# Two weight units' low halves computed on GpSimd instead of VectorE, in the first block's output projection

## What is computed

```python
def first_block(x, ...):
    h = x
    for layer in range(DEPTH):
        u = rms_norm(h, g_mix[layer])
        if layer % 2 == 0:      # 8 latent-attention heads and 8 stick-breaking heads
            h = h + mla_stick_breaking_mixer(u, ..., ev_w_out[i])
        else:
            h = h + chunk_band_mixer(u, od_w_qkv[i], od_rel_bias[i], od_w_out[i])
        u = rms_norm(h, g_ffn[layer])
        h = h + swiglu(u, w_gate[layer], w_up[layer], w_down[layer])
    return rms_norm(h, g_final)

# the end of mla_stick_breaking_mixer
    return jnp.concatenate([o_a, o_b], axis=-1) @ w_out
```

## Time and profile before

| what | value |
|---|---|
| median of 3 runs | 1110.11 us (1110.09 to 1110.68) |
| the profiled execution | 1109.47 us, its span 1107.7 us |
| mean granted TensorE clock | 0.991 |
| TensorE busy | 1078.0 us, 97% of the span |
| VectorE busy | 755.3 us, 68% |
| ScalarE busy | 578.0 us, 52% |
| GpSimd busy | 220.9 us, 20% |

### The profile page before, as it was taken

The page is one execution under the profiler, slowest core; times in us unless marked ns, Lnnn a source line. Parts: engine busy times, 40 slices in busy tenths (PEclk is TensorE's granted clock), DMA queues, the critical chain, the costliest instruction groups (busy, mean ns, idle before and its releaser), DMA issues.

```text
span 1107.7 us, 22257 instructions
## 1 busy us (share of the span) xinstructions
PE 1078.0 (97%) x8781; PEld 1053.5 (95%) x8781; DVE 755.3 (68%) x1233; ACT 578.0 (52%) x852; POOL 220.9 (20%) x202
## 2 busy tenths in 40 slices
PE   7998999999999999999999999999999989999997
PEld 7997999999999999999999899998899989999997
DVE  6677575555757766656555678987986657887652
ACT  5667554444545554644444544446666355555542
POOL 1431030000222110300000277785450000000000
PEclk9999999999999999999999999999999989999999
DMA  8734266657675343566555554453334534554451
GB/s 270 212 105 153 80 193 194 197 175 220 204 223 186 129 139 100 187 193 201 161 186 191 171 153 152 140 166 114 115 123 146 181 123 152 193 188 155 158 180 39
DMA packets 187941, 181.36 MB, mean 164 GB/s; under 512 B 17951, under 2 KB 186284, under 8 KB 187867
## 3 DMA queue, kind: packets, MB, share of 16 engines
q1 hardware_dynamic: 187323, 178.23, 50.9%
q0 software_dynamic: 544, 2.10, 0.7%
HBM read 179.27 MB, written 1.05 MB: 163 GB/s over the span
## 4 chain that ended last, share of the span: by engine, by line
PE 91%; DVE 4%; ACT 3%; issue 1%; DMA 0%; DVEq 0%; SPq 0%; ACTq 0%
PE ps L555 28%; PE ps L557 27%; PE ps L556 27%; DVE w_lo L394 1%; ACT w_hi L378 1%; PE ps L1981 1%; PE ps L2165 1%; PE ps L2103 1%; PE ps L1988 1%; PE ps L2172 1%; PE ps L2001 0%; PE ps L2000 0%; PE ps L1822 0%; PE ps L2127 0%; PE ps L1785 0%
## 5 line engine op out<-in xcount | busy, mean ns | idle before, releaser
L394 DVE TENSOR_TENSOR w_lo<-raw,w_hi 128x2048 fp32r<-128x2048 f32 (+3 forms) x157 | 333.4, 2137 | 137.6 <-ACT w_hi L378 137.4
L378 ACT ACTIVATE w_hi<-raw 128x2048 fp32r<-128x2048 f32 (+3 forms) x182 | 316.1, 1753 | 35.4 <-PE ps L557 25.3
L555 PE MATMUL ps<-u_hi,w_hi 128*128 128x256 f32 x944 | 265.1, 281 | 2.8 <-DVE w_lo L2343 2.3
L556 PE MATMUL ps<-u_lo,w_hi 128*128 128x256 f32 x944 | 262.4, 278 | 0.0
L557 PE MATMUL ps<-u_hi,w_lo 128*128 128x256 f32 x944 | 262.4, 278 | 0.0
L555 PE MATMUL ps<-m_hi,w_hi 128*128 128x258 f32 (+2 forms) x792 | 231.4, 292 | 6.6 <-DVE m_lo L524 4.2
L556 PE MATMUL ps<-m_lo,w_hi 128*128 128x258 f32 (+2 forms) x792 | 226.6, 286 | 0.0
L557 PE MATMUL ps<-m_hi,w_lo 128*128 128x258 f32 (+2 forms) x792 | 226.5, 286 | 0.0
L555 PEld LDWEIGHTS ps<-u_hi,w_hi 128*128 128x128 f32 x944 | 178.7, 189 | 4.0 <-DVE w_lo L2343 2.7
L556 PEld LDWEIGHTS ps<-u_lo,w_hi 128*128 128x128 f32 x944 | 178.6, 189 | 0.2
L557 PEld LDWEIGHTS ps<-u_hi,w_lo 128*128 128x128 f32 x944 | 178.6, 189 | 0.0
(11 more groups left out here) (364 smaller groups left out, 1681.0 us busy)
## 6 DMA issues: line engine op xcount, KB each, us to landing
raw<-in_w_in SPq DMA_DIRECT2D x24, 1024.0 KB, 5.3
raw<-in_w_gate SPq DMA_DIRECT2D x22, 1024.0 KB, 5.3
raw<-in_w_up SPq DMA_DIRECT2D x22, 1024.0 KB, 5.4
raw<-in_ffn_up SPq DMA_DIRECT2D x22, 1024.0 KB, 5.1
raw<-in_w_down SPq DMA_DIRECT2D x16, 768.0 KB, 4.6
raw<-in_od_w_qkv SPq DMA_DIRECT2D x12, 1024.0 KB, 5.2
raw<-in_w_down SPq DMA_DIRECT2D x16, 640.0 KB, 4.3
raw<-in_ev_w_in SPq DMA_DIRECT2D x7, 1024.0 KB, 10.1
```

Of the source, the lines that this page charges most:

```text
L378: nc.scalar.activation(w_hi[t % RING][:, 0:n], raw[t % RAW][:, 0:n], ACT.Copy).then_inc(hi_done, 1)
L394: nc.vector.tensor_tensor(w_lo[t % RING][:, 0:n], raw[t % RAW][:, 0:n], w_hi[t % RING][:, 0:n].bitcast(F32), ALU.subtract).then_inc(lo_don ...
L555: nc.tensor.matmul(out_ap, a_h, b_h, start=start and n == 0, stop=False)
L556: nc.tensor.matmul(out_ap, a_h, b_l, start=False, stop=False)
```

## The change

The table of VectorE loses the entries that make the low halves of units 15 and 16. GpSimd makes them instead, by the function that it already uses in the second block, behind its last copies of rotated queries (`cat`) and ahead of `fold_squares`. VectorE waits for `lo_done` of unit 16 before it makes unit 17, since the count must go up in order.

```diff
@@ split_lo
         nc.vector.wait_ge(hi_done, turn * ph.body + (t + 1))
-        if t == POOL_LO.stop:
+        if t in (OUT0_LO.stop, POOL_LO.stop):
             nc.vector.wait_ge(lo_done, t)
@@
+    OUT0_LO = range(ph_out0.u0 + 2, ph_out0.u0 + 4)
     POOL_LO = range(ph_mix.u0 + AHEAD, ph_wo.u0 + AHEAD)
@@
-    FM_HI, FM_LO = {174: 12, 178: 13, 194: 14}, {176: 12, 186: 13, 202: 14}
+    FM_HI, FM_LO = {174: 12, 178: 13, 194: 14}, {176: 12}
@@ block.gpsimd
         for m in range(4, MLA_H):
             cat(m)
+        for t in OUT0_LO:
+            split_lo_pool(t)
         fold_squares("ffn0", T1)
```

## The result

The changed kernel is slower: median 1112.2 us against 1109.95 us (20 runs of each, beside each other), ratio 1.0022 with a 95% interval of 1.0013 to 1.0030, that is +1.4 to +3.3 us. The prediction said 1111.5 us, 1.4 us more than before.

A forecast was written before the change was run, and what follows sets the result against it. TensorE, 97% busy, was taken as the bound. Unit 15's +0.8 and unit 16's +1.05 us gave +1.85, milder cases about +0.5; the chosen +1.4 on 1109.47 gave 1110.9, plus 0.64 for the median 1111.5, range 1109.7 to 1114.2.

The forecast's parts named there:

- What bounds the kernel: TensorE, 97% busy; in the stretch of the change it waits for `o_lo` 0.36 us at 119.03, about 0.25 at 125.50.
- the upper case: Unit 15 with head 11's first `tensor_scalar` held too: TensorE waits 0.85 us at 113.16, 2.0 us in all at 119.
- The lateness of the halves costs nothing: GpSimd's low halves of units 15 and 16 finish well before TensorE's first uses at 122.17 and 133.38; cost nothing.
- Gain without side effects, 0.25 us, at most 0.6: Splits removed from VectorE: TensorE's wait at 125.50 goes, 0.25 us; at most 0.6 if the 0.36 went too.
- Line 2438 is held for a whole piece, the second of a pair surely: VectorE's `tensor_scalar` pair beside GpSimd: second held a whole piece, first by a gap's remainder; bounds nothing and 1.04 us each.
- Line 2429 "held to the end of the running piece": VectorE's negated maxima (128x2) beside GpSimd: taken as held until the running piece ends; bounds nothing and 1.04 us.
- Unit 15: +0.8 worked, bounds 0 to 2.0: VectorE held beside unit 15's pieces: head 12's exponentials and TensorE at 119.03 come 0.8 us late; bounds 0 to 2.0.
- Unit 16: +1.05, bounds -0.25 to +1.4: VectorE held beside unit 16's pieces: TensorE's wait at 125.25 becomes 1.3 us for 0.25, +1.05; bounds -0.25 to +1.4.
- The size against 0.2%: Whole kernel: changes under 0.2% (2.2 us) can't be told from none; chances slower 0.22, faster 0.02, within 0.76.
- Rival 2, the lock doesn't bite: VectorE's small instructions slip between GpSimd's pieces: -0.25, at most -0.6 us, 1109.5 to 1110.2; chance 0.18.
- Rival 3, a clock fall caused by longer waits: Held VectorE plus TensorE's clock falling after longer waits: 5.1 us with one fall, 1113.5 to 1115.2; chance 0.22.
- Wrong if the shift changes later, where nothing was edited.: Behind the stage, from 134 us on, all starts should shift by one constant; otherwise the prediction is wrong.

The follow-up runs named there:

- the runs from PSUM: Changed kernel with latent-attention exponentials and row maxima kept in PSUM, run twice; ratios to the kernel before 0.9993 and 0.9995; control with VectorE's splits 1.0010.
- sixteen_pieces_hi_later: Changed kernel with sixteen GpSimd pieces per unit and ScalarE's high half of unit 16 at position 198 instead of 194; stage 27.04 us, ratio 0.9998 to before.
- one_piece: Changed kernel with GpSimd's half of each unit in one piece of 2048 columns instead of four of 512; stage 32.21 us, ratio 1.0047 to before.

## Why the prediction was right

**What bounds the kernel.** Right: the loss lies in the two waits for `o_lo` that were named, with a third, new one at 114.17 that the text had only for the upper case.

**The lateness of the halves costs nothing.** Right: no wait for `w_lo` in the stage, and the runs from PSUM show no cost of the move by itself, loads included.

**Gain without side effects, 0.25 us, at most 0.6.** -0.31 us with unit 16 moved away from all contention. The upper end was too low: it took the wait at 119.03 by its bracket, 0.36 us, where 0.52 us are lost, and `sixteen_pieces_hi_later` won 0.88 us in all.

**Line 2438 is held for a whole piece, the second of a pair surely.** Right as a mechanism and in the size, 1.0 us each, but not in the choice. Of head 11's pair it was the first that was held (1346 ns), until the last piece ended at 113.34, and the second was free (340 ns); with unit 15 alone it was the same, 1352 and 343 ns. Of head 14's both were held (1269 and 1390 ns), where I had the first free but for a moment. The prediction also says that the trace of before has no `tensor_scalar` beside a split. That holds only for those from SBUF to SBUF: line 2663, which reads PSUM, ran at 675.58 beside pieces from 675.22 to 680.24, and two of 144 columns took 0.78 us.

**Line 2429 "held to the end of the running piece".** Right, and it was the open one of the two bounds: 1131 ns for two numbers per partition. But it was head 11's instruction that was hit. Head 12's, which I had as held, took 0.17 us at 114.59, behind the last piece; so did head 15's at 125.76, which I had as held to 124.16. Head 11's came 0.35 us later after the restart than before, and so in the second piece; at the time of before it would have come at the end of the first. TensorE's clock had fallen 0.74 us after the restart (at 105.54) instead of 1.17 (at 105.47), and head 11's scores ended 0.36 us later. What is held depends on such moments. TensorE paid about one piece per unit in the profiles with four pieces and operands in SBUF, two for each unit; whether it would with other moments isn't shown.

**Unit 15: +0.8 worked, bounds 0 to 2.0.** Measured +1.22 in the changed kernel, +1.25 alone. **Unit 16: +1.05, bounds -0.25 to +1.4.** Measured +0.92, twice. The worked cases add up to 1.85, the stage gives 2.14 and the medians 2.25. The term that was mis-sized is the sum's last step: I took 1.4, "the value between", because some holds might not happen. The worked case was nearer. That it came so near is in part luck, since other instructions were held than the worked ones: for unit 15 two holds of about 1.0 us in place of one of 1.2 and one of 0.3, for unit 16 two holds of about 1.0 in place of one such, a short one, and one of head 15's negation. That a unit which slips one hold must meet the next, because the pieces follow one another without a gap, is an explanation that fits both units, not one that was tested.

**The size against 0.2%.** The measured 0.22% lies on the bound that parts "within" (0.76) from "slower" (0.22); the runs can't say on which side.

**Rival 2, the lock doesn't bite**: refuted by the durations. **Rival 3, a clock fall caused by longer waits**: it did not happen in the stage (1.00 from 109 on, waits of 0.99 us at most). In `one_piece` TensorE waited 1.28, 1.00 and 1.75 us there, and the clock stayed at 1.00 too.

**"Wrong if the shift changes later, where nothing was edited."** This sign did appear in the profile: 2.64 us at the stage's end, between -0.73 and 2.49 behind it, 1.0 at the end. The clock falls named above and the down projection named below account for three of the steps. Between 324 and 619 the changed kernel also won 1.5 us, at a granted clock of 1.00 in both, and no cause of that is shown. The medians of 20 runs, 2.25 us apart, agree with the stage and not with the end of that one execution; I take the sign as one that a single pair of profiles of this kernel can't give.

## What to carry to other kernels

An idle GpSimd beside a busy VectorE is not free capacity: ask which VectorE instructions will run beside its pieces, and whether they are of a kind that a trace shows as held, here `tensor_scalar` from SBUF. Those were held until the running GpSimd instruction ended, whether they had 2, 128 or 256 columns, so a negation of two numbers on the path can cost a microsecond. Where the move is wanted, cut GpSimd's instructions short, put them where VectorE reads PSUM only, or keep small operands in PSUM; the finest cut costs GpSimd 35% more time here, which nobody waited for.

## What the runs showed of the hardware

- A `tensor_scalar` of VectorE from SBUF to SBUF was held until the end of GpSimd's running `tensor_tensor`, even with 2 elements per partition: 1.13 us beside pieces of 512 columns, 3.18 and 3.35 us beside one of 2048. One that arrived as a piece ended went through: 0.17 us at 121.26 in the changed kernel, with the first piece from 120.05 and 1.25 us long. From PSUM it was not held: 0.16 us, with and without GpSimd. The reciprocal of two numbers per partition in SBUF took 0.17 us everywhere, beside GpSimd too. The Trainium skill (SBUF — State Buffer, "Who interferes with whom") names `tensor_scalar` among the operations that can take the shared ports, and says that an instruction of VectorE with at most one SBUF input, outside the two-port modes, doesn't contend. The runs from SBUF agree with the first and those from PSUM with the second; why the reciprocal is free isn't shown.
- About the same idle time of TensorE at the head of the stage, 2.28 to 2.32 us, was followed by a fall of the clock to half in ten of eleven profiles (1.7 us lost) and by none in one, with the same kernel doing both. The moment of the fall differed too: 1.17 us after the restart before, 0.74 us in the changed kernel.
- The down projection of layer 0 holds the same instructions in all kernels, at a granted clock of 1.00 and with one short wait of TensorE, for `w_lo` (0.23 us before, 0.55 in the changed kernel). From the first to the fourth of its results it took 46.1 us in two profiles, 47.1 in seven and 47.5 in two, with no value between. The changed kernel had 46.1 and the kernel before 47.5, which is 1.4 us of the span's difference. With unit 16 alone it was 47.5 and with unit 15 alone 46.1, so among these four it goes with unit 15's place; in the other seven it was 47.1 with unit 15 on either engine. There is one profile of most kernels, so whether it belongs to the kernel or to the execution isn't shown. The cause stays open.
